# A transformer pair on one core: two small attention stages merged, and the second block's modulation spread over both blocks

## The reference, cut to what matters

```python
def first_block(x, ...):
    for l in range(DEPTH):
        proj = rms_norm(x, ln1_gain[l]) @ w_in[l]
        o_nsa = nsa_mixer(...)
        o_mla = mla_mixer(...)
        o_ret = retention_mixer(...)
        x = x + concat(o_nsa, o_mla, o_ret) @ w_out[l]
        h = rms_norm(x, ln2_gain[l])
        x = x + square(relu(h @ w_up[l])) @ w_down[l]
    return rms_norm(x, final_gain)
```

## Time and profile before

| | us |
|---|---|
| median of 3 runs | 1237.38 (1236.75 to 1239.21) |
| the profiled execution | 1240.61 |
| its span, first to last instruction | 1238.8 |
| TensorE busy, share of the span | 1173.4, 95% |
| VectorE | 769.0, 62% |
| ScalarE | 545.7, 44% |
| GpSimd | 41.3, 3% |
| mean granted TensorE clock | 0.982 |

### The profile page before, as it was taken

How to read it: one execution, slowest core, us unless ns; L and a number is a source line. 1 busy time by engine, 2 the same in 40 slices (tenths; PEclk the granted TensorE clock), 3 DMA queues, 4 the chain that set the end, 5 groups by cost and what they waited for, 6 DMA issues and landing times. The chain is left out here.

```text
span 1238.8 us, 19484 instructions
## 1 busy us (share of the span) xinstructions
PE 1173.4 (95%) x7600; PEld 1016.0 (82%) x7600; DVE 769.0 (62%) x1454; ACT 545.7 (44%) x953; POOL 41.3 (3%) x45
## 2 busy tenths in 40 slices
PE   7988999999999998999999999899999999999996
PEld 6876868988987885877999899798887888988865
DVE  4574635655555464646787888679966644653474
ACT  4533534544444442634444444353547421533362
POOL 1000000000000000000100000000210000000000
PEclk9999989999999998799999999999999999999998
DMA  9538064555555546154555565333341022473101
GB/s 351 193 115 339 2 248 160 189 186 184 190 170 175 180 154 245 62 200 146 179 193 185 170 201 193 123 122 106 101 115 30 18 69 68 88 265 103 34 2 51
DMA packets 51647, 182.92 MB, mean 148 GB/s; under 512 B 17636, under 2 KB 30308, under 8 KB 31972
## 3 DMA queue, kind: packets, MB, share of 16 engines
q1 hardware_dynamic: 51556, 181.68, 44.0%
HBM read 178.78 MB, written 2.89 MB: 147 GB/s over the span
## 5 line engine op out<-in xcount | busy, mean ns | idle before, releaser
L219 DVE TENSOR_TENSOR w_lo<-ring,w_hi 128x1024 fp32r<-128x1024 f32 x264 | 322.1, 1223 | 249.0 <-ACT w_hi L213 247.0
L213 ACT CAST w_hi<-ring 128x1024 fp32r<-128x1024 f32 x264 | 275.2, 1051 | 355.6 <-PE banks L250 343.5
L250 PE MATMUL banks<-f_hi,w_hi 128*128 128x256 f32 x512 | 144.8, 283 | 0.5 <-DVE f_lo L352 0.5
L250 PE MATMUL banks<-f_hi,w_lo 128*128 128x256 f32 x512 | 145.0, 283 | 0.0
L250 PE MATMUL banks<-f_lo,w_hi 128*128 128x256 f32 x512 | 144.4, 282 | 0.0
L250 PE MATMUL banks<-w_hi,u_hi 128*128 128x512 f32 x256 | 101.1, 395 | 0.0
L250 PE MATMUL banks<-w_lo,u_hi 128*128 128x512 f32 x256 | 101.0, 395 | 0.0
L250 PE MATMUL banks<-w_hi,u_lo 128*128 128x512 f32 x256 | 101.0, 394 | 0.0
L281 PE MATMUL banks<-ident 128*128 128x128 f32 x750 | 93.4, 279 | 6.7 <-PEq L298 5.7
L281 PEld LDWEIGHTS banks<-ident 128*128 128x128 f32 x750 | 88.3, 193 | 14.0 <-issue 12.2
L250 PEld LDWEIGHTS banks<-f_hi,w_hi 128*128 128x128 f32 x512 | 96.7, 189 | 1.3 <-DVE f_lo L352 0.8
(11 more groups left out here) (365 smaller groups left out, 2299.7 us busy)
## 6 DMA issues: line engine op xcount, KB each, us to landing
ring<-in_w_up SPq DMA_DIRECT2D x32, 1024.0 KB, 5.2
ring<-in_w_down SPq DMA_DIRECT2D x32, 1024.0 KB, 5.1
ring<-in_w_in SPq DMA_DIRECT2D x24, 1024.0 KB, 5.1
ring<-in_ab_ada SPq DMA_DIRECT2D x12, 1024.0 KB, 6.4
ring<-in_cd_ada SPq DMA_DIRECT2D x12, 1024.0 KB, 5.7
ring<-in_cd_in SPq DMA_DIRECT2D x12, 1024.0 KB, 6.3
ring<-in_w_out SPq DMA_DIRECT2D x8, 1024.0 KB, 7.6
ring<-in_ab_in SPq DMA_DIRECT2D x16, 512.0 KB, 4.7
```

The costliest lines, as they stand in the source:

```text
L213: nc.scalar.copy(w_hi[:, n % PARTS, :], part_source(key, q)).then_inc(hi_ready, 1)
L219: nc.vector.tensor_tensor(w_lo[:, n % PARTS, :], part_source(key, q), w_hi[:, n % PARTS, :].bitcast(F32), ALU.subtract).then_inc(part_read ...
L250: mm = nc.tensor.matmul(dst, a, b, start=first_one and i == 0, stop=last_one and i == 2, skip_group_check=shares_bank)
```

## The change

It does six things at once.

1. `compressed_attention`, `retain` and the `transpose_groups` of the MLA heads become one stage, `compress_and_retain`, ahead of `attend`. The values are centered at the end of `project_and_prepare`, the gate is multiplied by its gain in `small_products`.
2. Layer 0 does three adaptation slabs of "ab" and layer 1 the other three: one in `transpose_heads`, one in `small_products`, one in the merged stage, right behind the scores. Each block of conditions is turned one stage later: four blocks in `small_products`, eight in the merged stage. The six slabs of "cd" move into the second block: two in `prepare_axial_heads`, one in its `transpose_groups`, three in `finish_conv_and_gate`, in the place of the fillers.
3. `turn_mixed` splits the first part of `w_out` or `ab_out` behind its first chunk; `ab_in` no longer splits two parts of `ab_out` ahead.
4. `out_project` loses the turned conditions, the biases and scales, and the seven fillers at its start.
5. The middle `final_norm` is made part of the norm of `project_and_convolve` (gain loaded in `feed_forward`, 34 fillers for twice 24).
6. Two memsets clear only the padding of the convolution's input.

The diff, cut to its core:

```diff
-LAYER_SLABS = [("w_in", W_IN_SLABS), ("cmp_k", 1), ("cmp_v", 1), ("small", 1), ("adapt0", 1), ("adapt1", 2),
-               ("adapt3", 3), ("w_out", 2), ("ffn", 16)]
+LAYER_SLABS = [("w_in", W_IN_SLABS), ("ada_turn", 1), ("cmp_k", 1), ("cmp_v", 1), ("small", 1), ("ada_small", 1),
+               ("ada_mix", 1), ("w_out", 2), ("ffn", 16)]
...
+SECOND_SLABS = [("ab_in", 6), ("cd_heads", 2), ("cd_turn", 1), ("cd_conv", 3), ("ab_out", 2), ("cd_in", 6), ("cd_out", 2)]
...
+def compress_and_retain(...):
+    scores_of(0)
+    scores_of(1)
+    ...
+    for h in range(2, RET_H):
+        scores_of(h)
+    adapt_products(pe, ada_key, 0, ADA)
+    values_of(0)
+    values_of(1)
+    pe.wait_ge(probs_ready, 1)
+    pe.wait_ge(kept, 1)
+    ...
+    for h in range(2, RET_H):
+        values_of(h)
+    pe.wait_ge(probs_copied, 2)
+    ...
+    for i in range(2):
+        mm = turn_conditions(adapted(1 + i), banks[:, ADA_TURNED, 16 * i:16 * (i + 1)])
+    for g, (blocks, _) in enumerate(groups):
+        if g >= 3:
+            pe.wait_ge(heads_copied, g - 2)
+        ...
...
 def prepare_axial_heads
     def _(sp):
+        load_behind(sp, "cd_heads", 2)
         sp.dma_start(rpb_rows[:, OFF_DIAGONAL:OFF_DIAGONAL + N_DC],
...
         spread_gates(pe, 0, 2, rows_ready)
-        keep_busy(7, 20)
+        for j in range(2):
+            adapt_products(pe, "cd_heads", j, 4 + j)
+        for j in range(2):
+            pe.wait_ge(kept, j + 1)
+            turn_conditions(cd_rows[:, j, :], banks[:, 6 + j, :]).then_inc(turned, 1)
...
 def finish_conv_and_gate
+    load_behind(sp, "cd_conv", 3)
...
-        keep_busy(7, 30)
-        pe.wait_ge(tanh_y_ready, 1)
-        keep_busy(7, 36)
+        for j in range(3):
+            adapt_products(pe, "cd_conv", j, 4 + j)
+        turn_conditions(cd_row, banks[:, 7, 0:16])
+        for j in range(3):
+            pe.wait_ge(kept, j + 1)
+            mm = turn_conditions(cd_rows[:, j, :], banks[:, 7, 16 * (j + 1):16 * (j + 2)])
+        keep_busy(4, 8)
...
 def turn_mixed
         nc.scalar.copy(hi[:, g * per:(g + 1) * per, 0:T * P], ...)
+        if g == 0:
+            split_hi(act, key, 0)
...
 def out_project
-        if kind is None:
-            keep_busy(6, 7)
-        else:
-            turn_conditions(pe, 1, 7, turned)
...
 def norm_programs
-        keep_busy(0, 24)
+        keep_busy(0, 24 if gain is None else 34)
...
 def transpose_groups
-        pe.wait_ge(copied1, 1)
-        keep_busy(1, busy)
+        if burst_bank < len(groups):
+            pe.wait_ge((copied0, copied1)[burst_bank % 2], burst_bank // 2 + 1)
+        adapt_products(pe, key, 0, burst_bank)
```

More of the change, by code:

```diff
@@ L231, in build_program @@
         next_key["w_out", DEPTH - 1], next_key[CTX_GLU] = CTX_GLU, ("ffn", DEPTH - 1)
+        TURN_AHEAD = [("w_out", layer) for layer in range(DEPTH)] + ["ab_out"]
         def split_own(split, engine, key, q):
-            if key not in next_key.values() or q >= AHEAD:
+            if q >= (1 if key in TURN_AHEAD else AHEAD if key in next_key.values() else 0):
                 split(engine, key, q)
@@ L252, in multiply, with adapt_products @@
             return mm
[L254 to L259, removed]
+        def adapt_products(pe, key, j, bank, signal=True):
+            for h in range(2):
+                i = first[key] + 2 * j + h
                 w = ring[:, i % SLOTS, :].rearrange("p (k n) -> p k n", k=KC // 2)
@@ L356, in on_vector @@
                     return
-                square_on_vector()
-                dve.wait_ge(norm_rstd, 1)
-                for n in others:
+                if gain is not None:
+                    two_norms_on_vector(dve)
+                else:
+                    square_on_vector()
+                    dve.wait_ge(norm_rstd, 1)
+                for n in (others if gain is None else ()):
                     t = tiles[n]
@@ L379, in on_gpsimd @@
             def on_gpsimd(pool):
+                if gain is not None:
+                    two_norms_on_gpsimd(pool)
+                    return
                 step = InOrder(pool, norm_step)
@@ L500, in products_done, with transpose_groups @@
             engine.wait_ge(part_used, first_part[key] + 4 * (s + 1))
-        def transpose_groups(groups, busy, loads=()):
-            with stage("turned", "copied0", "copied1", "tables_here") as (
-                    turned, copied0, copied1, tables_here), nc.Block() as block:
+        def transpose_groups(groups, burst):
+            key, burst_bank, rows = burst
+            with stage("turned", "copied0", "copied1") as (turned, copied0, copied1), nc.Block() as block:
                 @block.sync
                 def _(sp):
[L510 to L513, removed]
+                    load_behind(sp, key, 1)
                 @block.tensor
@@ L1289, in mixers @@
                             causal, plain_weigh(NSA_H * HD + h * HD, (0, 1))))
[L1290 to L1291 removed]
+                    attend(units, (probs, probsT, nmax, total, inverse))
                 pos_i = local.enter_context(nc.sbuf_tensor("pos_i", [P, TT], I32))
@@ new lines, in _ @@
+                    nc.scalar.copy(pT[:, 2 * BANK:3 * BANK], banks[0:N_CMP, 0, :]).then_inc(probs_copied, 1)
+                    act.wait_ge(ret_values, RET_H)
+                    for t in range(TT):
+                        nc.scalar.activation(sq[:, t, :], retained(t), ACT.Square).then_inc(squared, 1)
+                    for g, (_, copies) in enumerate(groups):
+                        act.wait_ge(heads_turned, g + 1)
+                        for copy in copies:
+                            last = copy(nc.scalar, banks[:, TURNED[g % 3], :])
+                        last.then_inc(heads_copied, 1)
```

430 lines of the change are left out of this document (231 added, 199 removed).

## The result

| | before | after |
|---|---|---|
| times shown ahead of the prediction, median | 1237.38 us | |
| beside each other on one chip, median | 1238.3 | 1224.64 (1223.83 to 1226.62, 4 runs) |
| ratio of times, 95% interval | | 0.9875 [0.9844, 0.9906] |
| a second comparison (`e8_change_again`) | 1241.47 | 1229.56, ratio 0.9886 [0.9861, 0.9911] |
| profiled execution, its span | 1240.61, 1238.8 | 1226.62, 1224.8 |

The change makes the kernel faster, by some 14 us (14.0 between the two spans, 15.5 by the ratio), where 25.2 were forecast. The ratio puts it at 1221.9 us for the 1237.38 of before (1218.1 to 1225.7), so at the upper end of the forecast range, 1200 to 1223; the median of its own runs is 1.6 above that range.

A forecast was written before the change was run, and what follows sets the result against it. In small stages the barrier-to-barrier chain was taken as the bound, TensorE's busy share being partly filler. Layer 0 -15.5, layer 1 -16.2 and second block +6.5 gave -25.2 us from the 1237.38 median: 1212.5, range 1200 to 1223.

The forecast's parts named there:

- merged stage for two: Compressed attention with MLA transposes, and retention, become one 20.2 us stage: 16.3 us saved in layer 0, 17.0 in layer 1.
- centering as a tail: Centering the values at the end of `project_and_prepare`, where VectorE alone ends the stage: +1.9 us per layer.
- norms merged: Two norm stages become one ahead of the second block, 34 fillers covering the norm's own chain: -4.4 us.
- transposes of the axial heads: Second block's head transposes: a burst and a copy in place of three fillers, +1.8 us.
- 1.2 GHz at the attention's start (attention): Slow clock after TensorE's idle 10 us: +3 us for transposes, burst and first attention units, between 0 and 6.
- finish: `finish_conv_and_gate`: VectorE's last product and 0.5 us of biases and scales end it instead of fillers, -1.7 us.
- The queue of `prepare_axial_heads`: SP issues four ring loads ahead of the `rpb_rows` load, delaying the skew write and barrier: +10.1 us, bounds +3.8 and +13.
- The sign of being right named in the prediction: In `prepare_axial_heads`: SP's skew write near 15 us behind the stage's start, no compute engine active before the barrier.
- Rival B: Clock low more often, at stage ends where fillers were: 4 us more in each layer, 1221 us; chance 0.15.
- rival C: Clock stays up: 3.7 us in layer 1's attention and about 3 per `w_out` start return, 1203 to 1206; chance 0.12.
- Rival D: Low clock from `prepare_axial_heads` lasts through attention into `ab_out`: slower than before, 1246 us; chance 0.03.
- E: The merged stage's burst waits for its slab's load, 2 to 3 us per layer, 1218 us; chance 0.05.

The follow-up runs named there:

- e8_change_again: The changed kernel run once more, unedited, beside the kernel before: 1229.56 us for 1241.47, ratio 0.9886.
- e11: The changed kernel with the three centering instructions moved to the head of the merged stage's VectorE queue: ratio 0.9841 to the kernel before, 1221.57 us.
- e5: The changed kernel with the two norms as separate stages again: ratio 0.993 to the kernel before, 1230.82 us.
- e1: The changed kernel with the `rpb_rows` load ahead of the four ring loads on SP's queue: ratio 0.9865 to the kernel before, 1224.57 us.
- e2: As e1, with the skew write issued by SP in the second block's attention stage: ratio 0.9755 to the kernel before, 1210.64 us.
- e3: The changed kernel with 32 fillers instead of 8 behind the last product of w_in: ratio 0.9908 to the kernel before, 1229.73 us.
- e6: The changed kernel with 8 more fillers ahead of the finish stage's turned conditions: ratio 0.9919 to the kernel before, 1230.01 us.
- e7: The changed kernel with 12 fillers ahead of the merged stage's compressed values, in each layer: ratio 0.9912 to the kernel before, 1229.8 us.

## Why the prediction was right in sign and wrong in size

All lengths from one profile each; what the clock moves between executions has just been shown.

| step (layer 0 / layer 1) | predicted | measured |
|---|---|---|
| merged stage for two | -16.3 / -17.0 | -12.6 / -14.8 |
| centering as a tail | +1.9 / +1.9 | +1.8 / +1.9 |
| `attend` | -0.5 / -0.5 | -0.8 / -4.5 |
| head transposes | +0.4 / +0.4 | +0.2 / +2.9 |
| `small_products` | +1.0 / +1.0 | +0.9 / +0.9 |
| to the first product of w_out | -2.0 / -2.0 | -1.8 / -2.1 |
| rest of `out_project` | 0 / 0 | -0.6 / -0.7 |
| sum, first block | -15.5 / -16.2 | -12.8 / -16.4 |
| norms merged | -4.4 | -4.1 |
| `prepare_axial_heads` | +10.1 | +10.55 |
| transposes of the axial heads | +1.8 | +6.9 |
| 1.2 GHz at the attention's start (attention) | +3 in all | +2.7 |
| finish | -1.7 | -0.5 |
| `ab_out` up to its first product | -0.5 | +0.7 |
| the rest, `cd_out` in it | -1.8 | -1.1 |
| sum, second block | +6.5 | +15.2 |

The measured steps add up to -14.0, which is the difference between the spans; the long product stretches between them add nothing. The forecast steps add up to -25.2, and taken from 1237.38 that is 1212.2, not the 1212.5 of the prediction.

**Right.** The terms that were instruction counts times a row's duration hit within 0.3 us: the tail of centering, which e11 confirms by taking it out; `small_products`; the slab products that start at once; the two norms, confirmed by e5. The queue of `prepare_axial_heads`, the part that spoke against the change, came out at +10.55 for +10.1, and it was shown by e1 to be SP's order: with the small load first the stage is about as long as before the change, 10.2 us for 10.04. That it came so near is partly luck. The last of the four ring loads landed 17.8 us into the stage, where the sum had 15.7 (933.7 less 918.04): the first landed 5.1 us after its issue, the others 2.5 to 2.9 us apart. And the skew write was issued 0.6 us behind that landing, where the sum had 2.8. The two misses, +2.1 and -2.2 us, cancel. The sign of being right named in the prediction, a write near 15 us behind the stage's start, does not fit its own sum, which has it at 18.5; it came at 18.4.

**Wrong, first: the clock inside and behind the small stages.** The merged stage of 20.2 was summed with every row at full clock. In layer 0 it took 23.86, above the 23 that the prediction had named as a sign of being wrong, though its last work was ScalarE's copies, as expected. In layer 0 TensorE's progress was as summed up to the compressed values, and what came then ran at 1.2 GHz; in layer 1 a first stretch of it fell into the scores and the burst (2.52 us for 1.92). That is 3.7 and 2.2 us here, and 2.2 and 3.6 in the second profile. An estimate from the windows, as if all of the stage went with the clock: 23.86 less half of 10.0 us, or 22.39 less half of 6.7, is 18.9 and 19.0, so that the sum at full clock was itself some 1 us long. (Its last gap was put at 0.7 to 1.1 us by the bracket of the 928.08 row, which reads 1.77; here it is 1.41.) Rival B had the mechanism (1.2 GHz more often, 4 us per layer, 1221) but put it behind idle gaps; it came as well inside the merged stages, where TensorE was never idle, so the prediction's reading that only the idle stretch matters is not borne out. B's 1221 lies beside the measured 1221.9, but that is luck in part, since B has no term for what SP does behind the skew write. The same failure makes +2.5 in layer 1's transposes, +1.2 in the finish stage and +1.2 in `turn_mixed`, and rival C's gain of 4.0 in layer 1's attention stands against it. That the extra comes from the granted clock is shown by the records; what in the new order brings it is not: wide fillers, more fillers and another place for the burst all left it there.

**Wrong, second: what is queued behind the moved write.** The term "Transposes of the axial heads: a burst and a copy for three fillers, +1.8" counted the burst on TensorE and ScalarE but not its two ring loads on SP, which stand behind the skew write. The compute engines are done at 911.5 and SP at 915.2; with the write elsewhere (e2) the stage falls by 3.6, to 7.2. The rest of this row's miss, 1.5, goes with 1.2 GHz over the transposes (3.71 us for 2.37), so that with the attention's 2.7 the +3 became 4.2. Before the change no load followed the write in that stage, so the cost was in no row.

**Wrong, third, small: the finish stage.** The sixth half came 1.9 us late on TensorE; the cover named for it, VectorE's chain, held. But the stage had eight fillers behind the turned conditions, and at 0.235 us a record they ended it, not VectorE.

Rival D did not happen: the 1.2 GHz of the idle stretch ended by 908, came again between 914 and 915, in the wait behind SP, and ended by 926. The longest stretch of before had lasted 13.7 us (497.9 to 511.6), a little more than the 13 that stand against D. E did not either: no wait for the slab stands in the merged stage.

## What to carry to other kernels

When a load or a write is moved onto a queue, walk that queue to the end of the next stage, too: a large write with many small packets can keep the issuing queue from its next issue, and a barrier waits for that queue as for any engine. Put a small load whose landing is waited for ahead of ring loads, and a write that nobody needs soon where its queue is empty. And where TensorE meets 1.2 GHz in small stages, sum them at both clocks: the forecast of full speed is then the favourable end, not the value (none of 26 merged stages ran at 2.4 GHz throughout), and one profile tells only one draw.

## What was not expected of the hardware

- The issue of two ring loads held SP for 9.4 us past the release of the second half, behind a skew write issued 7.5 us before, and for 0.4 without it. It ended when a certain part of the write's packets was through: with 825 to 843 and then 333 to 344 of 3584 left, in nine profiles.
- The same program ran its merged stage in 22.39 and in 23.86 us, and variants that differ from it only in the second block in up to 26.8, with other granted clocks and no idle time of TensorE inside the stage; over 15 runs of the kernel before, 0.012 of mean clock went with 11.2 us.
- 1.2 GHz came in a stage where TensorE had been busy without a gap for more than 10 us (104.16 to 116), and more fillers (e3, e6, e7) didn't keep it away.
- GpSimd's first step of the merged norm, on 2 columns, took 1.29 us beside a busy VectorE (below). The norm's own chain, put at 6.7, ended only at 774.5, 8.2 us into the stage and behind its 34 fillers (7.83 us): their cover is used up.

```profile
768.51 1.29 POOL L401 TENSOR_SCALAR rstd<-sums 128x2 f32<-128x2 f32 x1 [203.14 <-ACT proj_ab L389]
```
